# Strassen's block algorithm for the MLP's down product in a two-layer fp32 kernel on one core

## The chip, the core and the metric

The kernel runs on one core of a Trainium2 chip: TensorE (matmuls into PSUM), VectorE, ScalarE and GpSimd, each with its own instruction queue, and SyncE, whose queue issues most of the loads. The engines wait for each other through semaphores only. The metric is the time of one execution on the device in microseconds (us).

## What is computed

A block of an mLSTM mixer, stick-breaking attention and an MLP, then a block of sparse attention, on 512 tokens of width 1024 in fp32. The change touches the MLP of the first block alone:

```python
D_MODEL, SEQ, D_FF = 1024, 512, 4096
...
h2 = rms_norm(x, norm_mlp_g[l])
x = x + jnp.square(jax.nn.relu(h2 @ w_up[l])) @ w_down[l]
```

The result must have fp32's accuracy. The kernel reaches it with operands in a rounded format (fp32r): every matrix is split into a rounded part "hi" and the rest "lo", and a product is hi·hi + hi·lo + lo·hi, three matmuls.

## The kernel before

All weights are read as slabs of 1 MB, numbered through the program: 1024 rows x 256 columns, or (wide) 512 rows x 512 columns, a half of K. SyncE loads slab n into `w_raw[n % 2]` (L918 and L944), ScalarE rounds it into `w_hi[n % 2]` (`split_hi`, L550), VectorE forms the rest in `w_lo[n % 2]` (`split_lo`, L558: w_raw - w_hi), and TensorE uses both. Two slabs are in the works: slab n + 1 is split while TensorE works on n, and its rounding waits until TensorE has done with slab n - 1.

The MLP (`N_MLP`) runs in four rounds, one for each 1024 of the 4096 hidden columns, as a hardware loop on each engine (L944, L1134, L1450, L1695). A round has

- four up slabs. `mm_tile` (L581) makes two tiles of 128 hidden columns x 512 tokens of each, 24 matmuls a tile (8 steps of K, 3 parts), into the two banks of `ps_g` in turns. A tile is evacuated by ScalarE's Relu into `ev_t` (L732), VectorE's product with the tile itself, which gives the square, into `relu_t` (L819), ScalarE's rounding into `up_hi` (L734) and VectorE's rest into `up_lo` (L822). Only then is its bank free for the next tile but one.
- four wide down slabs, two halves of K for each 512 of the 1024 output columns. `mm_half` (L604) has the up activations as the stationary operand and adds into four banks, one for each 128 tokens; after the second half VectorE adds the bank to `x_sb` (L826).

Each engine does its work in program order: `act_slab` and `dve_slab` do the split of slab n + 1 first and then the evacuations of slab n. GpSimd has nothing to do in the MLP.

Behind the last round ScalarE squares the four blocks of 128 tokens of `x_sb` with a running sum (L886), VectorE forms the reciprocal root and the normalised `xn` (L900 to L908), and TensorE transposes it (`feature_tiles`, L632) for the next layer. Blocks 0 to 2 and block 3 are two parts of that.

## Time and profile before

| | us |
|---|---|
| median of 3 runs | 1376.48 |
| lowest, highest | 1375.53, 1377.55 |
| the profiled execution | 1374.61 |
| its span | 1372.9 |
| TensorE busy in the span | 1333.3 |
| VectorE, ScalarE, GpSimd busy | 669.1, 618.9, 201.9 |

The profile records one execution, instruction by instruction. Its page gives each engine's busy time, the granted clock of TensorE in 40 slices, the chain of waits that ended last, the costliest groups of instructions and the DMA issues; its trace can be asked for windows and timelines. A matmul is recorded for 0.39 us and the next starts 0.23 us behind it, since they are pipelined: their price is the distance between starts. "L558" is a line of the kernel. "1.26 <-ACT w_hi" behind an instruction is the engine's idle time before it and what ended it. An instruction that is held up after its start has the waiting time in its own duration.

### The profile page before, as it was taken

The numbers are of one execution on the slowest core, as the hardware profiler recorded it, in microseconds if no ns is written. First come the engines' busy times: TensorE is split into PE (matmuls) and PEld (weight loads), VectorE is DVE, ScalarE is ACT, GpSimd is POOL, SyncE is SP. The second block draws the span as 40 slices with busy tenths as digits, with TensorE's granted clock in tenths as the row PEclk, the third lists the DMA queues.
The fourth block names the chain that finished last, engine by engine and source line by source line (L and its number), as shares of the span: only waits on it lengthen the run. The fifth ranks groups of instructions, "written<-read, shape, count | busy, mean of one in ns | idle before, by whom it ended". The sixth has DMA issues, their size and how long they took to land.

```text
span 1372.9 us, 18095 instructions
## 1 busy us (share of the span) xinstructions
PE 1333.3 (97%) x7245; PEld 1115.1 (81%) x7245; DVE 669.1 (49%) x1093; ACT 618.9 (45%) x961; POOL 201.9 (15%) x265
## 2 busy tenths in 40 slices
PE   5999999999999999999999999999999999999998
PEld 4887777777778887888888888788899998989876
DVE  4753444344444545434434344431256767776563
ACT  5254554446766424323323223244334666666232
POOL 1101333261000000000000000002712333332000
PEclk9999999999999999999999999999999999999999
DMA  8747534494424322322232322272512222222321
GB/s 170 111 111 115 77 78 81 105 196 99 61 54 59 93 96 71 110 92 92 95 105 89 109 92 92 92 218 77 131 39 67 81 70 70 63 85 78 99 71 62
DMA packets 94807, 128.81 MB, mean 94 GB/s; under 512 B 5840, under 2 KB 70464, under 8 KB 94737
## 3 DMA queue, kind: packets, MB, share of 16 engines
q1 hardware_dynamic: 88528, 108.70, 32.1%
q0 software_dynamic: 6064, 18.83, 5.2%
...
## 4 chain that ended last, share of the span: by engine, by line
PE 86%; DVE 5%; DMA 4%; POOL 2%; ACT 2%; issue 1%; SPq 0%; DVEq 0%
PE ps_g L581 44%; PE ps_g L604 13%; PE ps_z L604 12%; PE ps_z L1236 3%; PE ps_z L1273 2%; PE ps_t L1308 2%; DMA w_raw<-in_w_in 2%; DMA bc<-stat_rows_dram 2%; PE ps_t L1045 1%; PE ps_t L1083 1%; DVE w_lo L558 1%; PE ps_z L1097 1%; POOL y_f L1907 1%; PE ps_t L1158 1%; PE ps_z L1121 1%
## 5 line engine op out<-in xcount | busy, mean ns | idle before, releaser
L558 DVE TENSOR_TENSOR w_lo<-w_raw,w_hi 128x2048 fp32r<-128x2048 f32 (+1 forms) x96 | 220.9, 2302 | 302.0 <-ACT w_hi L550 302.0
L581 PE MATMUL ps_g<-act_hi,w_hi 128*128 128x512 f32 x784 | 309.4, 395 | 7.8 <-DVE act_lo L697 5.3
L581 PE MATMUL ps_g<-act_hi,w_lo 128*128 128x512 f32 x784 | 306.3, 391 | 0.0
L581 PE MATMUL ps_g<-act_lo,w_hi 128*128 128x512 f32 x784 | 305.9, 390 | 0.0
L550 ACT ACTIVATE w_hi<-w_raw 128x2048 fp32r<-128x2048 f32 (+1 forms) x96 | 182.2, 1898 | 210.1 <-PE ps_g L604 189.0
L581 PEld LDWEIGHTS ps_g<-act_hi,w_hi 128*128 128x128 f32 x784 | 147.7, 188 | 41.0 <-DVE w_lo L558 5.8
L581 PEld LDWEIGHTS ps_g<-act_hi,w_lo 128*128 128x128 f32 x784 | 147.5, 188 | 31.3
L581 PEld LDWEIGHTS ps_g<-act_lo,w_hi 128*128 128x128 f32 x784 | 147.6, 188 | 29.5
L581 PE MATMUL ps_g<-w_hi,act_hi 128*128 128x256 f32 x320 | 93.4, 292 | 0.0
L581 PE MATMUL ps_g<-w_lo,act_hi 128*128 128x256 f32 x320 | 90.3, 282 | 0.0
L581 PE MATMUL ps_g<-w_hi,act_lo 128*128 128x256 f32 x320 | 90.2, 282 | 0.0
L1939 POOL TENSOR_SCALAR cmp_in_k<-pairk,vec 128x124 f32<-128x124 f32 x16 | 11.7, 749 | 518.0 <-ACT pairk L747 518.0
L1507 ACT ACTIVATE probs<-probs,rneg 128x128 f32<-128x128 f32 (+3 forms) x128 | 70.4, 551 | 13.8 <-DVE rneg L1761 12.8
L1959 POOL TENSOR_TENSOR q_parts<-qn,q_parts 64x512 fp32r<-64x512 f32 x32 | 42.0, 1312 | 139.6 <-ACT q_parts L1487 139.3
L581 PEld LDWEIGHTS ps_g<-w_hi,act_hi 128*128 128x128 f32 x320 | 61.1, 191 | 0.2 <-issue 0.2
L581 PEld LDWEIGHTS ps_g<-w_lo,act_hi 128*128 128x128 f32 x320 | 61.2, 191 | 0.0
L581 PEld LDWEIGHTS ps_g<-w_hi,act_lo 128*128 128x128 f32 x320 | 61.0, 191 | 0.0
L732 ACT ACTIVATE ev_t<-ps_g 128x512 f32<-128x512 f32 x32 | 19.2, 600 | 85.7 <-PE ps_g L581 85.7
L1757 DVE CUSTOM_DVE_ANT_0 probs<-ps_z,tile_t 128x128 f32<-128x128 f32 (+3 forms) x128 | 55.0, 485 | 5.7 <-PE ps_z L1236 3.2
L604 PE MATMUL ps_g<-w_hi,act_hi 128*128 128x512 f32 x128 | 49.9, 390 | 0.7 <-DVE act_lo L695 0.7
L819 DVE TENSOR_TENSOR relu_t<-ev_t,ps_g 128x512 f32<-128x512 f32 x32 | 22.0, 688 | 58.6 <-ACT ev_t L732 58.6
L604 PE MATMUL ps_z<-w_hi,act_hi 128*128 128x512 f32 x128 | 50.4, 394 | 0.0
...
## 6 DMA issues: line engine op xcount, KB each, us to landing
w_raw<-in_w_in SPq DMA_DIRECT2D x32, 1024.0 KB, 9.6
w_raw<-in_nsa_w_in SPq DMA_DIRECT2D x22, 1024.0 KB, 5.2
w_raw<-in_w_up SPq DMA_DIRECT2D x16, 1024.0 KB, 5.4
w_raw<-in_w_down SPq DMA_DIRECT2D x16, 1024.0 KB, 5.1
...
w_raw<-in_w_out SPq DMA_DIRECT2D x4, 1024.0 KB, 5.1
w_raw<-in_nsa_w_out SPq DMA_DIRECT2D x4, 1024.0 KB, 5.0
```

The source lines that it names most:

```text
L550: nc.scalar.activation(slab_view(w_hi[b], n), slab_view(w_raw[b], n), ACT.Copy).then_inc(hi_done, 1)
L558: nc.vector.tensor_tensor(slab_view(w_lo[b], n), slab_view(w_raw[b], n), slab_view(w_hi[b], n).bitcast(F32), ALU.subtract).then_inc(lo_don ...
L581: mm = nc.tensor.matmul(o, stationary, moving, start=(k == 0 and j == 0), stop=(k == KT - 1 and j == 2))
L604: mm = nc.tensor.matmul(bank(t), act[:, k, m], w[:, k - k0, :], start=(k == 0 and j == 0), stop=(k == KT - 1 and j == 2))
L732: nc.scalar.activation(ev_t[:, g, :], ps_g[:, g, :], ACT.Relu).then_inc(ev_act, 1)
L819: nc.vector.tensor_tensor(relu_t[:, g, :], ev_t[:, g, :], ps, ALU.mult)\
L1236: mm = nc.tensor.matmul(ps_z[:, at:at + w], q_parts[u % 2][:, b * P:(b + 1) * P], keys[u // 4 % 2][:, 0:w], start=(j == 0), stop=(j == 1))
L1273: mm = nc.tensor.matmul(ps_z[64 * e:64 * e + 64, CAUSAL + at * P:CAUSAL + (at + 1) * P], values[:, s, g * DH:(g + 1) * DH], probs_t[:, blo ...
L1308: mm = nc.tensor.transpose(ps_t[:, at:at + P], probs[u % 2][:, ROWS_AT[b] + s * P:ROWS_AT[b] + (s + 1) * P], ident)
L1507: ins = nc.scalar.activation(p, p, ACT.Exp, bias=rneg[:, u % 2, b:b + 1], accum_out=rsum[:, u % 2, b:b + 1])
L1757: ins = nc.vector.tensor_tensor_reduce(probs[u % 2][:, at:at + w], ps_z[:, at:at + w], tile_t[u % 2][:, S - w:S], 1.0, -3.0e38, ALU.add, A ...
L1959: nc.gpsimd.tensor_tensor(q_parts[u % 2][64 - half:128 - half, :], qn[half:half + 64, 4 * (h // 8) + h % 4, :], q_parts[u % 2][half:half + ...
```

## The change

The down product of each round is done with Strassen's algorithm in Winograd's form. The round's up activations A (512 tokens x 1024) and weights B (1024 x 1024) are cut into four blocks each: A11, A12, A21, A22 (first index: half of the tokens; second: half of K) and B11 to B22 (half of K; half of the output columns). Instead of 8 block products there are seven:

- M1 = A11·B11, M2 = A12·B21
- S1 = A21 + A22, S2 = S1 - A11, S3 = A11 - A21, S4 = A12 - S2
- T1 = B12 - B11, T3 = B22 - B12, T2 = T3 + B11, T4 = B21 - T2
- M5 = S1·T1, M4 = A22·T4, M6 = S2·T2, M7 = S3·T3, M3 = S4·B22

The output's blocks are x11 += M1 + M2, x12 += M1 + M6 + M5 + M3, x21 += M1 + M6 + M7 + M4, x22 += M1 + M6 + M7 + M5. (T4 and M4 have their signs such that these hold.) The products run in the order M1, M2, M5, M4, M6, M7, M3, each with 24 matmuls (2 blocks of 128 tokens, 4 steps of K, 3 parts).

Each product has a slab of weights of its own that is split as before, so a round has 11 slabs, four for up and seven for down, in place of 8. The four raw down slabs are loaded into buffers of their own (`down_raw`). New work in a round:

- GpSimd: T3, T1 and T2 (2048 elements in each partition), released by the split of up slab 2, by the one before, and by the split of M1; S3, S2, S4 (1024 elements), released by `mixed_1` and then by one another; six additions of 512 elements to `x_sb` behind M6 and M7.
- VectorE: S1 (`mix1`, 1024 elements), T4 (2048), the rests of S1 to S4 (1024 each), 12 additions of 512 elements from PSUM (8 before), seven splits (4 before). The rests of A11 and A12 alone are half as wide at the first four up tiles.
- ScalarE: seven roundings of weights (4 before), two copies of M1 out of PSUM, the roundings of S1 to S4.

The hardware loops are written out. The blocks of tokens are normalised for the next layer in the order 2, 3, 0, 1.

```diff
+M1, M2, M5, M4, M6, M7, M3 = range(7)
+PRODUCTS = 7
...
+        up_raw = [sb(f"up_raw{j}", [P, HALF_K, S], at=arena + 2 * K16 + 8192 * j) for j in range(2)]
+        down_raw = [sb(f"down_raw{i}", [P, HALF_K, WIDE], at=arena + 3 * K16 + 8192 * i) for i in range(4)]
+        mix1 = sb("mix1", [P, HALF_K, HALF_S], at=arena + 5 * K16)
+        prod1 = sb("prod1", [P, 2, WIDE], at=arena + 5 * K16 + 4096)
+        prod16 = sb("prod16", [P, 2, WIDE], at=arena + 5 * K16 + 8192)
+        prod167 = sb("prod167", [P, 2, WIDE], at=arena + 5 * K16 + 12288)
...
+        NORM_BLOCKS = ((0, 1, 2, 3), (0, 1, 2, 3), (2, 3, 0, 1))
...
+        def down_operand(p):
+            j = 0 if p in (M1, M5, M6, M3) else 1
+            half = slice(0, HALF_S) if p in (M1, M2, M6, M7) else slice(HALF_S, S)
+            return (up_parts[j][0][:, :, half], up_parts[j][1][:, :, half])
+        def down_bank(p, i):
+            return {M1: ps_z[:, 512 * i:512 * i + 512], M2: ps_z[:, 512 * i:512 * i + 512],
+                    M5: (ps_z, ps_t)[i][:, 1024:1536], M3: (ps_z, ps_t)[i][:, 1024:1536],
+                    M4: ps_g[:, i, :],
+                    M6: ps_t[:, 512 * i:512 * i + 512], M7: ps_t[:, 512 * i:512 * i + 512]}[p]
...
+            def down_product(q, p):
+                n = N_MLP + MLP_SLABS * q + 4 + p
+                up0 = tile_of[n - p - 4]
+                pe.wait_ge(lo_done, n + 1)
+                hi, lo = down_operand(p)
+                wh, wl = slab_view(w_hi[n % 2], n), slab_view(w_lo[n % 2], n)
+                if p in (M1, M2):
+                    for k in range(HALF_K):
+                        wait_tile_free(pe, up0 + HALF_K * p + k)
+                elif p != M4:
+                    pe.wait_ge(mix_lo, 4 * q + {M5: 1, M6: 2, M7: 3, M3: 4}[p])
+                for i in range(2):
+                    if p == M1 and q:
+                        pe.wait_ge(prod_added, added(q - 1, M2, i))
+                    elif p == M2:
+                        pe.wait_ge(prod_copied, 2 * q + i + 1)
+                    elif p == M5 and q:
+                        pe.wait_ge(prod_added, added(q - 1, M3, i))
+                    elif p == M6 and q:
+                        pe.wait_ge(prod_added, added(q - 1, M7, i))
+                    elif p == M7:
+                        pe.wait_ge(prod_added, added(q, M6, i))
+                    elif p == M3:
+                        pe.wait_ge(prod_added, added(q, M5, i))
+                    first, last_ = p not in (M2, M7, M3), True
+                    for k in range(HALF_K):
+                        m = slice(i * P, (i + 1) * P)
+                        for j, (act, w) in enumerate(((hi, wh), (hi, wl), (lo, wh))):
+                            mm = nc.tensor.matmul(down_bank(p, i), act[:, k, m], w[:, k, :],
+                                                  start=(first and k == 0 and j == 0),
+                                                  stop=(k == HALF_K - 1 and j == 2), skip_group_check=True)
+                    mm.then_inc(prod_done, 1)
...
+            def mixed_hi(q, s):
+                src, dst = ((mix1[:], up_parts[0][0][:, :, HALF_S:S]),
+                            (up_raw[0][:, :, 0:HALF_S], up_parts[0][0][:, :, 0:HALF_S]),
+                            (up_raw[0][:, :, HALF_S:S], up_parts[1][0][:, :, 0:HALF_S]),
+                            (up_raw[1][:, :, 0:HALF_S], up_parts[0][0][:, :, HALF_S:S]))[s]
+                if s == 0:
+                    act.wait_ge(mixed_1, q + 1)
+                else:
+                    act.wait_ge(mixed_up, 3 * q + (2, 1, 3)[s - 1])
+                    act.wait_ge(prod_done, prod_count(q, (M1, M2, M5)[s - 1], 1))
+                nc.scalar.copy(dst, src).then_inc(mix_hi, 1)
+            for q in range(4):
+                n = N_MLP + MLP_SLABS * q
+                for j in range(4):
+                    act_slab(act, n + j)
+                for p in range(PRODUCTS):
+                    split_hi(act, n + 4 + p + 1)
+                    if p == M1:
+                        for i in range(2):
+                            act.wait_ge(prod_done, prod_count(q, M1, i))
+                            if q:
+                                act.wait_ge(prod_added, added(q - 1, M7, i))
+                            nc.scalar.copy(prod1[:, i, :], down_bank(M1, i)).then_inc(prod_copied, 1)
+                            if i == 0:
+                                mixed_hi(q, 0)
+                    elif p in (M5, M4, M6):
+                        mixed_hi(q, {M5: 1, M4: 2, M6: 3}[p])
+            def x_there(b):
+                if b >= 2:
+                    act.wait_ge(prod_merged, 6 * 3 + 2 + 2 * (b - 1))
+                else:
+                    act.wait_ge(prod_added, added(3, M3, b))
+            act_rms(act, 2, x_there)
...
+            def mixed_lo(q, s):
+                src, j, half = ((mix1[:], 0, slice(HALF_S, S)),
+                                (up_raw[0][:, :, 0:HALF_S], 0, slice(0, HALF_S)),
+                                (up_raw[0][:, :, HALF_S:S], 1, slice(0, HALF_S)),
+                                (up_raw[1][:, :, 0:HALF_S], 0, slice(HALF_S, S)))[s]
+                dve.wait_ge(mix_hi, 4 * q + s + 1)
+                nc.vector.tensor_tensor(up_parts[j][1][:, :, half], src, up_parts[j][0][:, :, half].bitcast(F32),
+                                        ALU.subtract).then_inc(mix_lo, 1)
+            def add_product(q, p, i):
+                dve.wait_ge(prod_done, prod_count(q, p, i))
+                ps = down_bank(p, i)
+                if p in (M6, M7):
+                    if p == M6:
+                        dve.wait_ge(prod_copied, 2 * q + i + 1)
+                        if q:
+                            dve.wait_ge(prod_merged, 6 * (q - 1) + 2)
+                    elif q:
+                        dve.wait_ge(prod_merged, 6 * q)
+                    dst = (prod16 if p == M6 else prod167)[:, i, :]
+                    nc.vector.tensor_tensor(dst, prod1[:, i, :], ps, ALU.add).then_inc(prod_added, 1)
+                    return
+                x = x_block(*{M2: (0, 0), M5: (1, 1), M4: (1, 0), M3: (0, 1)}[p], i)
+                if p == M3:
+                    dve.wait_ge(prod_merged, 6 * q + i + 1)
+                elif p in (M5, M4) and q:
+                    dve.wait_ge(prod_merged, 6 * q)
+                nc.vector.tensor_tensor(x, x, ps, ALU.add).then_inc(prod_added, 1)
+            for q in range(4):
+                n = N_MLP + MLP_SLABS * q
+                for j in range(4):
+                    dve_slab(dve, order, n + j)
+                dve.wait_ge(ev_dve, dve_count[tile_of[n + 4]])
+                nc.vector.tensor_tensor(mix1[:], up_raw[0][:, :, HALF_S:S], up_raw[1][:, :, HALF_S:S], ALU.add)\
+                    .then_inc(mixed_1, 1)
+                for p in range(PRODUCTS):
+                    split_lo(dve, n + 4 + p + 1)
+                    if p == M1:
+                        mixed_lo(q, 0)
+                        dve.wait_ge(mixed_w, 3 * q + 3)
+                        dve.wait_ge(lo_done, n + 4 + M2 + 1)
+                        nc.vector.tensor_tensor(down_raw[1][:], down_raw[1][:], down_raw[0][:], ALU.subtract)\
+                            .then_inc(mixed_b21, 1)
+                    else:
+                        add_product(q, p, 0)
+                        if p in (M5, M4, M6):
+                            mixed_lo(q, {M5: 1, M4: 2, M6: 3}[p])
+                        add_product(q, p, 1)
...
+            for q in range(4):
+                n = N_MLP + MLP_SLABS * q
+                b11, b12, b22 = (down_raw[i][:] for i in (0, 2, 3))
+                t3 = slab_view(w_raw[raw_of[n + 4 + M7]], n + 4 + M7)
+                a11, a21 = up_raw[0][:, :, 0:HALF_S], up_raw[0][:, :, HALF_S:S]
+                a12 = up_raw[1][:, :, 0:HALF_S]
+                for i in (3, 2):
+                    pool.wait_ge(down_in[i], 16 * (q + 1))
+                pool.wait_ge(lo_done, n + 3)
+                nc.gpsimd.tensor_tensor(t3, b22, b12, ALU.subtract).then_inc(mixed_w, 1)
+                pool.wait_ge(down_in[0], 16 * (q + 1))
+                pool.wait_ge(mixed_w, 3 * q + 1)
+                nc.gpsimd.tensor_tensor(b12, b12, b11, ALU.subtract).then_inc(mixed_w, 1)
+                pool.wait_ge(lo_done, n + 4 + M1 + 1)
+                pool.wait_ge(mixed_w, 3 * q + 2)
+                nc.gpsimd.tensor_tensor(b11, t3, b11, ALU.add).then_inc(mixed_w, 1)
+                pool.wait_ge(mixed_1, q + 1)
+                nc.gpsimd.tensor_tensor(a21, a11, a21, ALU.subtract).then_inc(mixed_up, 1)
+                pool.wait_ge(mixed_up, 3 * q + 1)
+                nc.gpsimd.tensor_tensor(a11, mix1[:], a11, ALU.subtract).then_inc(mixed_up, 1)
+                pool.wait_ge(mixed_up, 3 * q + 2)
+                nc.gpsimd.tensor_tensor(a12, a12, a11, ALU.subtract).then_inc(mixed_up, 1)
+                for i in range(2):
+                    pool.wait_ge(prod_added, added(q, M6, i))
+                    x = x_block(0, 1, i)
+                    nc.gpsimd.tensor_tensor(x, x, prod16[:, i, :], ALU.add).then_inc(prod_merged, 1)
+                for i in range(2):
+                    pool.wait_ge(prod_added, added(q, M7, i))
+                    for column in range(2):
+                        x = x_block(1, column, i)
+                        nc.gpsimd.tensor_tensor(x, x, prod167[:, i, :], ALU.add).then_inc(prod_merged, 1)
```

How instructions move. VectorE, from the fourth up slab of a round to the down product; before (`w_lo` is the rest of a weight slab; REGISTER_ALU belongs to the loop):

```order
L558 TENSOR_TENSOR w_lo_57<-w_raw_53,w_hi_55 128x2048 [waits hi_done]
L668 REGISTER_ALU
L819 TENSOR_TENSOR relu_t<-ev_t,ps_g 128x512 [waits ev_act]
L668 REGISTER_ALU
L822 TENSOR_TENSOR up_lo<-relu_t,up_hi 128x512 [waits ev_act]
L557 REGISTER_ALU
L558 TENSOR_TENSOR w_lo_56<-w_raw_52,w_hi_54 128x2048 [waits hi_done]
L557 REGISTER_ALU
L558 TENSOR_TENSOR w_lo_57<-w_raw_53,w_hi_55 128x2048 [waits hi_done]
```

and after, in the same place (down_raw_101, 102, 103 hold B11, B21 and B12, later T2, T4 and T1):

```order
L886 TENSOR_TENSOR up_lo<-up_raw_100,up_hi 128x512 [waits ev_act]
L1915 TENSOR_TENSOR mix_105<-up_raw_99,up_raw_100 128x1024 [waits ev_dve]
L615 TENSOR_TENSOR w_lo_56<-down_raw_102,w_hi_54 128x2048 [waits hi_done]
L1886 TENSOR_TENSOR up_lo<-mix_105,up_hi 128x4x256 [waits mix_hi]
L1923 TENSOR_TENSOR down_raw_102<-down_raw_102,down_raw_101 128x2048 [waits lo_done,mixed_w]
L615 TENSOR_TENSOR w_lo_57<-down_raw_103,w_hi_55 128x2048 [waits hi_done]
L1908 TENSOR_TENSOR x_sb<-x_sb,ps_z 128x512 [waits prod_done] x2
```

Between the last evacuation of an up tile and the split of the third product's weights stand now, besides the split of the second product's, S1, the rest of S1 and T4. GpSimd, in the place of the MLP, before:

```order
L1844 AFFINE_SELECT sp_t<-sp_t 128x128 [waits b_sp] x2
L1844 AFFINE_SELECT sp_t<-sp_t 128x128 x2
L1939 TENSOR_SCALAR cmp_in_k<-pairk,vec 128x124 [waits tile_free0,tile_free1]
L1939 TENSOR_SCALAR cmp_in_k<-pairk,vec 128x124 x15
L1939 TENSOR_SCALAR cmp_in_v<-pairv,vec 128x124 [waits cmp_ready,tile_free0,tile_free1]
```

and after, the first of four rounds (up_raw_99 holds A11 and A21, up_raw_100 A12 and A22, w_raw_53 T3, prod_107 M1 + M6, prod_108 M1 + M7, to which M6 is added in PSUM):

```order
L2076 AFFINE_SELECT sp_t<-sp_t 128x128 x2
L2174 TENSOR_TENSOR w_raw_53<-down_raw_104,down_raw_103 128x2048 [waits lo_done,down_in2,down_in3]
L2177 TENSOR_TENSOR down_raw_103<-down_raw_103,down_raw_101 128x2048 [waits mixed_w,down_in0]
L2180 TENSOR_TENSOR down_raw_101<-w_raw_53,down_raw_101 128x2048 [waits mixed_w,lo_done]
L2182 TENSOR_TENSOR up_raw_99<-up_raw_99 128x4x256 [waits mixed_1]
L2184 TENSOR_TENSOR up_raw_99<-mix_105,up_raw_99 128x4x256 [waits mixed_up]
L2186 TENSOR_TENSOR up_raw_100<-up_raw_100,up_raw_99 128x4x256 [waits mixed_up]
L2190 TENSOR_TENSOR x_sb<-x_sb,prod_107 128x512 [waits prod_added] x2
L2195 TENSOR_TENSOR x_sb<-x_sb,prod_108 128x512 [waits prod_added]
```

GpSimd, which had no instruction in the MLP, has twelve in each round.

## Rows read from the trace of the kernel before

**Rows 1.** The page, part 1: busy us (share of the span) xinstructions
```profile
PE 1333.3 (97%) x7245; PEld 1115.1 (81%) x7245; DVE 669.1 (49%) x1093; ACT 618.9 (45%) x961; POOL 201.9 (15%) x265
```

**Rows 2.** Window table inside the MLP: stretch, us, busy us (count) by engine
```profile
600.00:850.00 250.00, 250.00 (x1105) 207.01 (x1104) 100.14 (x93) 72.22 (x71) 0.00 (x0) 1.00 0.30 96
```

**Rows 3.** Chain of waits before the MLP: start us, us, what
```profile
519.34 5.44 PE ps_z L604 x24
```

**Rows 4.** Timeline between two MLP rounds: start us, us, engine, line, operation
```profile
625.92 0.39 PE L581 MATMUL ps_g<-act_hi,w_hi 128*128 128x512 f32 x1
626.12 1.92 ACT L550 ACTIVATE w_hi<-w_raw 128x2048 fp32r<-128x2048 f32 x1 [8.96 <-PE ps_g L604]
...
628.07 2.29 DVE L558 TENSOR_TENSOR w_lo<-w_raw,w_hi 128x2048 fp32r<-128x2048 f32 x1 [1.26 <-ACT w_hi L550]
```

**Rows 5.** Timeline, ScalarE then VectorE, end of a round's first up slab
```profile
637.00 0.60 ACT L732 ACTIVATE ev_t<-ps_g 128x512 f32<-128x512 f32 x1 [3.46 <-PE ps_g L581]
638.36 0.62 ACT L734 CAST up_hi<-relu_t 128x512 fp32r<-128x512 f32 x1 [0.75 <-DVE relu_t L819]
...
637.64 0.69 DVE L819 TENSOR_TENSOR relu_t<-ev_t,ps_g 128x512 f32<-128x512 f32 x1 [3.37 <-ACT ev_t L732]
...
640.83 2.29 DVE L558 TENSOR_TENSOR w_lo<-w_raw,w_hi 128x2048 fp32r<-128x2048 f32 x1 [1.13 <-ACT w_hi L550]
```

**Rows 6.** Lines that split weight slabs: count, ns least/median/most
```profile
L558 DVE TENSOR_TENSOR w_lo<-w_raw,w_hi x96: 1226/2293/3367, 17.3 to 1347.2; 128x2048 fp32r<-128x2048 f32 x94, 128x1024 fp32r<-128x1024 f32 x2
...
L550 ACT ACTIVATE w_hi<-w_raw x96: 1045/1916/1992, 15.3 to 1345.2; 128x2048 fp32r<-128x2048 f32 x94, 128x1024 fp32r<-128x1024 f32 x2
```

**Rows 7.** GpSimd's tensor_tensor by line: count, ns least/median/most, shape
```profile
L1888 POOL TENSOR_TENSOR den_sum<-den_sum,decay x8: 459/792/797, 130.3 to 241.6; 128x128 f32<-128x128 f32 x8
...
L1907 POOL TENSOR_TENSOR y_f<-y_f,bc x8: 1272/1516/3332, 275.5 to 301.3; 128x512 f32<-128x512 f32 x8
...
L1959 POOL TENSOR_TENSOR q_parts<-qn,q_parts x32: 1282/1291/1980, 1023.2 to 1256.9; 64x512 fp32r<-64x512 f32 x32
```

**Rows 8.** Timeline pieces, GpSimd and VectorE, at 277 to 301 us
```profile
277.25 1.78 DVE L1647 SCALAR_TENSOR_TENSOR q_b<-q_b,gq_s,bc 128x512 f32<-128x512 f32 x1
...
278.44 1.74 POOL L1907 TENSOR_TENSOR y_f<-y_f,bc 128x512 f32<-128x512 f32 x1
...
296.72 4.59 POOL L1907 TENSOR_TENSOR y_f<-y_f,bc 128x512 f32<-128x512 f32 x2
...
296.79 3.37 DVE L558 TENSOR_TENSOR w_lo<-w_raw,w_hi 128x2048 fp32r<-128x2048 f32 x1 [9.01 <-ACT w_hi L550]
...
297.98 3.33 POOL L1907 TENSOR_TENSOR y_f<-y_f,bc 128x512 f32<-128x512 f32 x1
```

**Rows 9.** Timeline at 1063 us: GpSimd beside a VectorE operation on PSUM
```profile
1061.83 2.63 POOL L1969 TENSOR_TENSOR k_lo<-ks,k_hi 64x512 fp32r<-64x512 f32 x2 [2.91 <-ACT k_hi L1500]
...
1063.30 0.69 DVE L1757 CUSTOM_DVE_ANT_0 probs<-ps_z,tile_t 128x512 f32<-128x512 f32 x1
```

**Rows 10.** The page, part 6: DMA issues, KB each, us to landing
```profile
w_raw<-in_w_down SPq DMA_DIRECT2D x16, 1024.0 KB, 5.1
```

**Rows 11.** TensorE's timeline after a gap; window table (PEclk third from the end)
```profile
20.44 0.47 PE L581 MATMUL ps_g<-act_hi,w_hi 128*128 128x512 f32 x1 [3.64 <-DVE act_lo L697]
...
21.46 0.59 PE L581 MATMUL ps_g<-act_lo,w_hi 128*128 128x512 f32 x1
...
24.83 0.43 PE L581 MATMUL ps_g<-act_hi,w_hi 128*128 128x512 f32 x1
...
20.00:24.00 4.00, 3.56 (x11) 0.69 1.02 77
```

**Rows 12.** Timeline, TensorE and ScalarE, at the end of the MLP rounds
```profile
886.82 0.39 PE L604 MATMUL ps_g<-w_hi,up_lo 128*128 128x512 f32 x1
...
888.15 1.04 ACT L886 ACTIVATE xn<-x_sb 128x1024 f32<-128x1024 f32 x1
...
889.30 0.55 PE L632 MATMUL ps_z<-cst,xn 128*128 128x128 f32 x3 [2.09 <-DVE xn L908]
```

More of the change, by code:

```diff
@@ L471, in program @@
             tile_of[n] = len(kinds)
+            if slabs[n][4] == "down":
+                continue
             if k_half(n) is None:
@@ L623, in feature_bank, with feature_tiles @@
             return (ps_z, ps_t)[k // 3][:, k % 3 * 512:(k % 3 + 1) * 512]
-        def feature_tiles(pe, n, src, block_ready, between=None, before=None):
+        def feature_tiles(pe, n, src, block_ready, between=None, before=None, blocks=range(TB), late=None):
             t0 = norm_tile_of[n]
```

292 lines of the change are left out of this document (179 added, 113 removed).

## The prediction

> **What bounds the kernel now.** I read the page first: TensorE is busy 97% of the span, VectorE 49%, ScalarE 45%, GpSimd 15% [rows 1]. Then the stretch that the change touches, the four MLP rounds from 538.7 us to 887 us. In the window table 250 us out of the middle of it are 250.00 us of TensorE work, with GpSimd at 0.00 and the granted clock at 1.00 [rows 2]. So TensorE alone sets the time here, at one tile of 24 matmuls in 5.44 us [rows 3], 0.2267 us a matmul; a round has 384 of them, 87.05 us.
>
> What keeps the other engines off the path is slack. At a slab's boundary ScalarE rounds the next weight slab (1.92 us) and VectorE then forms its rest (2.29 us); with the handovers the slab is ready 4.44 us behind the boundary (625.92 to 628.07 + 2.29 [rows 4]), while TensorE works 10.88 us on a slab. Behind an up slab its last tile is evacuated first (Relu 0.60, product 0.69, rounding 0.62 us, then a rest as long as the product) and the split runs from 636.80 (625.92 + 10.88) to 643.12, 6.32 us [rows 5]. ScalarE has up to 8.96 us to wait for TensorE [rows 4].
>
> **TensorE's part of the change.** Seen as blocks (tokens halved, K halved, output columns halved) the down product of a round is 8 block products of 24 matmuls (2 token tiles, 4 steps of K, 3 parts): 192. Seven block products are 168. So 24 matmuls, 5.44 us, leave each round and 21.8 us the kernel. The matmul has the same shape as before, hence its price.
>
> **The slack after it.** A product lasts 2 x 12 x 0.2267 = 5.44 us where a slab lasted 10.88. The pair of split halves still takes 4.44 us: 1.0 us of slack is left at each product instead of 6.4. So every further operation of VectorE and ScalarE in the product part has to be placed. Durations I use: 2048 elements 1.92 us on ScalarE and 2.29 on VectorE [rows 4]; 1024 elements 1.05 and 1.23 (the least of the two lines that split slabs, which are the half-width ones) [rows 6]; 512 elements 0.60 and 0.69 [rows 5].
>
> **GpSimd's operations.** Its tensor_tensor takes at least 0.46 us for 128 elements and 1.27 us for 512 [rows 7]: 0.19 us and 2.11 ns an element. Worked out from these: 1024 elements 2.35 us, 2048 elements 4.5 us. The trace has none so long; the slower end is the median of the 512-element line in the sparse attention, 1291 ns, at that rate throughout: 2.52 ns an element [rows 7], 2.6 and 5.2 us; the faster end has no fixed part, 2.11 ns throughout, 2.2 and 4.3 us. I take the line through the two minima, which are undisturbed. The Trainium skill (GPSIMD Engine Reference, Performance versus the Vector engine) gives 4497 ns for 2048 fp32 elements, no row here shows it; by it the sum would stay.
>
> **What decides: GpSimd and VectorE don't run side by side on these operations.** At 296 us GpSimd is in the midst of four multiplications of 512 elements. VectorE's split starts at 296.79, just behind one of them (296.72), and is recorded with 3.37 us instead of 2.29: it waits 1.08 us, until that one is done, then runs. GpSimd's next operation, begun at 297.98, takes 3.33 instead of 1.27: it waits 2.1 us until the split has ended at 300.16 [rows 8]. From 277.25 on the two alternate one by one: VectorE's 0.75 us operation is recorded with 1.78, and GpSimd's with 1.74, each behind one of the other engine [rows 8]. Whereas VectorE's operations with one operand in PSUM ran inside a GpSimd pair (1063.30, 0.69 us for 512 elements, no longer than elsewhere) [rows 9]. So: operations with two SBUF inputs exclude each other, whole instruction by whole instruction, in turns; adds from PSUM are free. The Trainium skill (SBUF — State Buffer, SBUF: two separate sides) calls it an exclusive lock and not a bandwidth split; these rows agree with it. If the ports were shared by bandwidth, as the skill's page says they are not, the sum would be that of rival A below.
>
> **The round, step by step**, in us from its first matmul; boundaries between engines 0.03 to 0.1.
> - Up part. GpSimd's first weight difference starts when slab 2 of the round is split: TensorE's tile 1 ends at 10.88, the split 6.2 later (a 256-wide rounding and rest are 0.2 shorter each), 17.1. It holds until 21.7 (4.5). VectorE's rest of tile 2 (ready 18.3) waits and runs to 22.1; the second difference runs 22.1 to 26.6; the rest of tile 3 waits from 23.7 to 26.6 and ends 27.05. TensorE needs that bank for tile 5 at 27.20: no stall, by 0.15 us. The third runs 39.2 to 43.7 behind M1's split and delays the rest of tile 6 to 44.4, that of tile 7 hardly (46.5). M1 starts on time at 43.52: 0.
> - M1 to M2. M2's split needs tile 7 evacuated first: VectorE's mix1 ends 47.75 (46.5 + 1.23), ScalarE's rounding of M2 47.7. M2 should start at 48.96. From 47.8 VectorE has in its queue: split M2 (2.29), rest of mix1 (1.23), difference for M4 (2.29), split M5 (2.29) = 8.1 us. GpSimd is released by mix1 at the same instant for its three sums of up activations, each waiting for the one before: 3 x 2.35 = 7.05 us. All seven have two SBUF inputs. In turns, whoever is first, all three GpSimd sums are done before split M5 starts: 47.8 + 8.1 + 7.05 = 62.95. M2 starts at 50.1 or, if GpSimd wins the first turn, at 52.5, and ends 55.5 or 57.9; M5 starts at 63.0 either way instead of 54.4. **Stall 8.6 us a round**, +34.4 us.
> - M5, M4, M6, M7, M3. VectorE's load per 5.44 us is split 2.29, rest 1.23, two adds 1.38 = 4.9 us. From M6's start T: split M7 to T + 4.44, add, rest to 6.4, GpSimd's first add to x (1.27) to 7.7, split M3 7.7 to 10.0, needed at 10.88; GpSimd to 11.25; two adds; one GpSimd add holds until 13.87, so the next slab's split ends 16.16, needed at 16.32. It fits, with 0.16 us: 0.
> - Loads. 8 MB a round as before, 5.1 us each [rows 10]; they are issued at the splits of the round before and land before use, also in the first round, where four of them are queued at once. 0.
>
> **The clock.** At 20.44 us TensorE had idled 3.64 us; between 21.46 and 24.83 only eight matmuls start, 0.42 us apart instead of 0.227, the lower of the two levels (granted clock 0.69 in 20 to 24 us) [rows 11]: 1.6 us lost. A gap of 7.5 us (or two, of 3.5 and 5) before M5 will do the same: +1.6 a round, +6.4 us. Bounds: 0, and 2 x 1.6 if both gaps do it.
>
> **The end of the rounds.** Now the squares of blocks 0 to 2 are done beside TensorE, and the first transpose starts 2.09 us after its last matmul (886.82 + 0.39 to 889.30) [rows 12]: VectorE's add 0.69, then 1.4 for mean, root, reciprocal and the first normalisation. After the change blocks 2 and 3 are complete only with GpSimd's six adds to x, of which the last ends 2.3 us behind M3's end (held once by the split of the next slab); then two squares (2 x 1.25: 1.04 [rows 12] and the reading of the sum) and the 1.4: first transpose 6.2 us behind. +4.1 us, once. At least 1.9 if nothing holds the adds.
>
> **Sum**, against the profiled execution (1374.6 us in all, its span 1372.9): -21.8 + 34.4 + 6.4 + 4.1 = +23.1. The three runs have their median 1.9 us above that execution, so 1376.5 + 23.1 = **1399.6 us**.
>
> **Rivals.**
> - A: the exclusion doesn't bite in this place (the sums find the gaps between VectorE's operations, or my reading of rows 8 holds for those forms only). Then split M5 ends at 47.8 + 8.1 = 55.9: stall 1.5 us a round, no clock loss, tail +1.9: -21.8 + 6 + 1.9 = -13.9, **1362.6 us, faster**. It decides below a stall of about 4.4 us a round (21.8 - 4.1 over four), that is with one GpSimd sum in the way, not three. For it: VectorE and ScalarE are half idle. Against: rows 8 show both engines waiting, to the hundredth.
> - B: only two of the three sums get in before split M5, or the clock doesn't fall: 2.35 x 4 = 9.4 less, or 6.4 less: 1390 to 1393. It needs VectorE to win two turns running; at 277.25 to 278.95 it won none.
> - C: GpSimd is at its slower rate. The first two differences then end 1.4 us later, tile 5 waits 1.3 us a round, the three sums 0.8 more: +8.4, **1408**. Double clock loss would add 6.4 to the forecast likewise.
> - D: the split of a further product comes late (slack 0.16 us behind M3): some tenths a round, within the range.
>
> **Chances.** Forecast with D 0.58, B 0.14, C and the double clock loss 0.18, A 0.10. Range 1384 to 1411: it takes in B and C with their bounds and leaves out A and a sum of all bad ends. A measurement of this kernel can tell about 0.2%, 2.7 us. Faster 0.10, same 0.02, slower 0.88.
>
> **What would show it.** In the profile after: tiles of 5.44 us still; per round two gaps of TensorE before M2 and before M5, together near 8.6 us, ended by VectorE's w_lo; recorded VectorE operations in that place longer than 2.29 by whole GpSimd operations, and GpSimd's 1024-element sums longer than 2.35; granted clock below 1 behind the gap; VectorE's busy time up far more than its elements. Wrong if w_lo stays 2.29 us beside a busy GpSimd (then A), if the gap stands at another product, or if the up tiles wait (then C).

## The result, and the profile after

The changed kernel takes **1398.74 us** (median of 4 runs, 1395.45 to 1400.6), the kernel before beside it 1377.01. The ratio is 1.0162, with a 95% interval from 1.0146 to 1.0177: slower, and 0.9 us from the predicted 1399.6. The difference of the two medians is +21.7 us where +23.1 was forecast; the kernel before ran 0.5 us above the 1376.5 that the forecast started from. The profiled execution took 1395.45 us, the shortest of the four, and its span is 1393.7.

The page, part 1, of the changed kernel (busy us, share of the span, instructions; compare [rows 1]):

```profile
PE 1324.2 (95%) x7149; PEld 1103.4 (79%) x7149; DVE 799.2 (57%) x1145; ACT 657.3 (47%) x997; POOL 347.8 (25%) x313
```

TensorE has 96 instructions fewer, as it should. VectorE's busy time is up by 130 us, and GpSimd's by 146. Since a waiting instruction has its wait in its duration, both are more than the new work.

The best measure of the change is a stretch that holds all of it and nothing else: from the MLP's first matmul to the first matmul of the next layer. TensorE's timeline of the kernel before, start us, us, then the instruction and its wait:

```profile
538.73 0.50 PE L581 MATMUL ps_g<-act_hi,w_hi 128*128 128x512 f32 x1 [0.80 <-DVE act_lo L697]
...
894.15 0.47 PE L581 MATMUL ps_g<-act_hi,w_hi 128*128 128x512 f32 x1 [0.89 <-DVE act_lo L697]
```

and of the changed one:

```profile
537.75 0.47 PE L638 MATMUL ps_g<-act_hi,w_hi 128*128 128x512 f32 x1 [0.89 <-DVE act_lo L759]
...
917.32 0.47 PE L638 MATMUL ps_g<-act_hi,w_hi 128*128 128x512 f32 x1 [0.89 <-DVE act_lo L759]
```

355.42 us before and 379.57 after: **+24.15**. What lies outside this stretch took 1017.5 us before and 1014.1 after, so that the two profiled executions are only 20.8 us apart. Over the profiled executions of all the kernels here, whose code doesn't differ there, it lies between 1014.1 and 1019.0. The missing 3.4 us are within that scatter of single executions, and the experiments below are compared by their stretch as well as by their time.

Where TensorE waited in the MLP of the changed kernel (waits of TensorE, 530 to 915 us: us in total, times, longest):

```profile
PE ps_z L1274 <- DVE w_lo L615: 28.6, 8, 6.4
PE ps_z L689 <- DVE xn L976: 7.9, 2, 5.7
PE ps_g L638 <- DVE up_lo L886: 1.1, 4, 0.3
```

Eight waits for a weight split, two a round, at M2 and at M5. In the second round (its first matmul starts at 629.45) TensorE's timeline has them so:

```profile
679.90 0.50 PE L1274 MATMUL ps_z<-w_hi,up_hi 128*128 128x512 f32 x1 [0.77 <-DVE w_lo L615]
...
692.02 0.79 PE L1274 MATMUL ps_z<-w_hi,up_hi 128*128 128x512 f32 x1 [6.37 <-DVE w_lo L615]
692.61 0.63 PE L1274 MATMUL ps_z<-w_lo,up_hi 128*128 128x512 f32 x1
693.03 0.63 PE L1274 MATMUL ps_z<-w_hi,up_lo 128*128 128x512 f32 x1
...
695.98 0.39 PE L1274 MATMUL ps_z<-w_hi,up_hi 128*128 128x512 f32 x1
```

M2 starts at 50.45 in the round (forecast 50.1, or 52.5) and M5 at 62.57 (forecast 63.0). Behind the second wait the matmuls start some 0.43 us apart (the first two 0.59) instead of 0.23, until 695.98. The windows of the same kernel (stretch, us, busy us of PE, PEld, DVE, ACT, POOL with counts, granted clock, DMA share, GB/s; compare [rows 2]):

```profile
540.00:900.00 360.00, 330.36 (x1409) 268.45 (x1408) 266.05 (x180) 136.12 (x133) 138.56 (x44) 0.96 0.26 83
...
692.00:696.00 4.00, 3.98 (x10) 3.15 (x11) 3.36 (x3) 0.00 (x0) 0.00 (x0) 0.51 0.67 219
```

The clock is 0.51 behind the gap, the lower of the two levels (1.2 GHz), and 0.96 in the mean of the MLP, where it was 1.00.

**Why the split is late** stands on the two other engines in the same place, VectorE first, then GpSimd:

```profile
676.35 1.22 DVE L1915 TENSOR_TENSOR mix<-up_raw,up_raw 128x1024 f32<-128x1024 f32 x1
677.56 2.29 DVE L615 TENSOR_TENSOR w_lo<-down_raw,w_hi 128x2048 fp32r<-128x2048 f32 x1
679.77 3.43 DVE L1886 TENSOR_TENSOR up_lo<-mix,up_hi 128x1024 fp32r<-128x1024 f32 x1
683.12 4.48 DVE L1923 TENSOR_TENSOR down_raw<-down_raw,down_raw 128x2048 f32<-128x2048 f32 x1
687.52 4.44 DVE L615 TENSOR_TENSOR w_lo<-down_raw,w_hi 128x2048 fp32r<-128x2048 f32 x1
...
677.65 4.47 POOL L2182 TENSOR_TENSOR up_raw<-up_raw 128x1024 f32<-128x1024 f32 x1 [3.99 <-DVE mix L1915]
682.19 3.25 POOL L2184 TENSOR_TENSOR up_raw<-mix,up_raw 128x1024 f32<-128x1024 f32 x1
685.53 4.28 POOL L2186 TENSOR_TENSOR up_raw<-up_raw,up_raw 128x1024 f32<-128x1024 f32 x1
```

Read them as one sequence of turns. VectorE's split of M2 comes first (2.29, unhindered). GpSimd's S3, begun at 677.65, waits for it until 679.8 and ends at 682.12. VectorE's rest of S1 (1.22 by itself, recorded with 3.43) waits for S3 and ends at 683.20; S2 waits for it, T4 (2.29 by itself, 4.48 here) for S2, S4 for T4, and the split of M5 (4.44) for S4. Seven operations, strictly in turns, from 677.56 to 691.96: 14.4 us. TensorE starts M5 0.06 us later.

### The profile page after: what moved, and what is told of

It is laid out like the page before. It is cut to its first block, busy times and chain, and to the rows that moved or that the text cites. A ratio compares the mean times of both kernels' runs of the same rounds, so it can differ in the third digit from the quotient of the medians.

```text
span 1393.7 us, 17752 instructions
## 1 busy us (share of the span) xinstructions
PE 1324.2 (95%) x7149; PEld 1103.4 (79%) x7149; DVE 799.2 (57%) x1145; ACT 657.3 (47%) x997; POOL 347.8 (25%) x313
## 4 chain that ended last, share of the span: by engine, by line
PE 81%; DVE 10%; ACT 3%; DMA 2%; issue 2%; POOL 1%; SPq 0%; DVEq 0%; ACTq 0%; POOLq 0%
PE ps_g L638 42%; PE ps_g L661 7%; PE ps_z L661 7%; PE ps_t L1274 4%; DVE w_lo L615 3%; PE ps_z L1387 3%; PE ps_z L1424 3%; PE ps_t L1459 2%; PE ps_z L1274 2%; DMA w_raw<-in_w_in 2%; PE ps_g L1274 2%; DVE down_raw L1923 1%; DVE up_lo L886 1%; PE ps_t L1156 1%; PE ps_t L1194 1%
## 5 line engine op out<-in xcount | busy, mean ns | idle before, releaser
L615 DVE TENSOR_TENSOR w_lo<-w_raw,w_hi 128x2048 fp32r<-128x2048 f32 (+1 forms) x84 | 196.6, 2340 | 230.0 <-ACT w_hi L607 230.0
L607 ACT ACTIVATE w_hi<-w_raw 128x2048 fp32r<-128x2048 f32 (+1 forms) x84 | 159.2, 1896 | 116.8 <-PE ps_g L661 62.1
L607 ACT ACTIVATE w_hi<-down_raw 128x2048 fp32r<-128x2048 f32 x24 | 46.0, 1916 | 71.5 <-PE ps_t L1274 47.3
L615 DVE TENSOR_TENSOR w_lo<-down_raw,w_hi 128x2048 fp32r<-128x2048 f32 x24 | 66.9, 2788 | 13.1 <-ACT w_hi L607 13.1
L1274 PE MATMUL ps_z<-w_hi,up_hi 128*128 128x512 f32 x96 | 42.1, 438 | 28.6 <-DVE w_lo L615 28.6
L886 DVE TENSOR_TENSOR up_lo<-up_raw,up_hi 128x256 fp32r<-128x256 f32 (+1 forms) x32 | 54.5, 1702 | 18.6 <-ACT up_hi L797 18.6
L2174 POOL TENSOR_TENSOR w_raw<-down_raw,down_raw 128x2048 f32<-128x2048 f32 x4 | 18.4, 4607 | 167.8 <-DVE w_lo L615 167.8
```

The lines of the kernel that those rows point to most:

```text
L607: nc.scalar.activation(slab_view(w_hi[b], n), slab_view(raw(n), n), ACT.Copy).then_inc(hi_done, 1)
L615: nc.vector.tensor_tensor(slab_view(w_lo[b], n), slab_view(raw(n), n), slab_view(w_hi[b], n).bitcast(F32), ALU.subtract).then_inc(lo_done, 1)
L886: nc.vector.tensor_tensor(up_parts[j][1][:, k, cols], up_raw[j][:, k, cols], up_parts[j][0][:, k, cols].bitcast(F32), ALU.subtract).then_i ...
L1274: mm = nc.tensor.matmul(down_bank(p, i), act[:, k, m], w[:, k, :], start=(first and k == 0 and j == 0), stop=(k == HALF_K - 1 and j == 2), ...
```

## Experiments

In 1 to 5 all else is as in the changed kernel; 6 and 7 change the rearranged kernel of 4. "Stretch" is the distance defined above, in one profiled execution of each.

| | median us | ratio to before, 95% interval | stretch us |
|---|---|---|---|
| before | 1376.05 to 1377.01 | | 355.42 |
| changed | 1398.74 | 1.0162 [1.0146, 1.0177] | 379.57 |
| sums on one element | 1364.48 | 0.9912 [0.9896, 0.9929] | 346.99 |
| memsets in their place | 1364.40 | 0.9915 [0.9898, 0.9932] | 345.74 |
| sums behind the split of M5 | 1376.09 | 0.9993 [0.9983, 1.0003] | 357.19 |
| rearranged | 1364.35 | 0.9913 [0.9897, 0.9930] | 345.50 |
| the same again | 1364.10 | 0.9914 [0.9897, 0.9930] | 345.54 |
| sums on VectorE | 1383.18 | 1.0058 [1.0042, 1.0073] | 365.83 |
| rearranged, other parts of the normalisation | 1363.97 | 0.9910 [0.9897, 0.9924] | 346.81 |
| rearranged, last additions on VectorE | 1364.94 | 0.9912 [0.9895, 0.9929] | 344.65 |

**1. The three sums made small.**

```diff
-nc.gpsimd.tensor_tensor(a21, a11, a21, ALU.subtract).then_inc(mixed_up, 1)
+nc.gpsimd.tensor_tensor(a21[:, 0:1, 0:1], a11[:, 0:1, 0:1], a21[:, 0:1, 0:1],
+                        ALU.subtract).then_inc(mixed_up, 1)
```

and likewise S2 and S4.

> The changed kernel with GpSimd's three sums of up activations (S3, S2, S4) done on one element in each partition in place of 1024; the rest of them is left out, every wait stays. Theory L (two-input operations of GpSimd and VectorE exclude each other whole, so the three sums lengthen VectorE's chain before the fifth matrix product M5 by their own 3 x 2.35 us): M5 starts 1.1 + 0.4 us late a round instead of about 8.6, the clock doesn't fall there, recorded w_lo of that place is 2.29 us: 1398.7 - 4 x 7.1 - 6.4 = about 1364 us, faster than before. Theory V (VectorE's own 8.1 us of queue and ScalarE's order behind it make the gap, GpSimd is beside the path): gap and time stay, 1394 to 1399.

Measured: 1364.48 us. Of the eight waits for `w_lo` only the four of 0.77 us at M2 are left. VectorE and GpSimd in the second round:

```profile
669.44 2.29 DVE L615 TENSOR_TENSOR w_lo<-down_raw,w_hi 128x2048 fp32r<-128x2048 f32 x1
671.65 1.22 DVE L1886 TENSOR_TENSOR up_lo<-mix,up_hi 128x1024 fp32r<-128x1024 f32 x1
672.79 2.29 DVE L1923 TENSOR_TENSOR down_raw<-down_raw,down_raw 128x2048 f32<-128x2048 f32 x1
674.99 2.28 DVE L615 TENSOR_TENSOR w_lo<-down_raw,w_hi 128x2048 fp32r<-128x2048 f32 x1
...
669.53 2.25 POOL L2182 TENSOR_TENSOR up_raw<-up_raw 128x1 f32<-128x1 f32 x1 [3.98 <-DVE mix L1915]
671.86 1.06 POOL L2184 TENSOR_TENSOR up_raw<-mix,up_raw 128x1 f32<-128x1 f32 x1
673.00 2.12 POOL L2186 TENSOR_TENSOR up_raw<-up_raw,up_raw 128x1 f32<-128x1 f32 x1
```

All that VectorE does has its own length again. GpSimd's subtractions of a single element still wait out each operation of VectorE (2.25, 1.06, 2.12 us). So the turns go by instruction, whatever its size. VectorE loses only as much as GpSimd holds, and the M5 wait is GpSimd's three sums. It doesn't yet tell whether GpSimd's being busy or its reading is what excludes.

**2. GpSimd busy, but without inputs.** Each sum is three memsets of its target, one after the other.

```diff
-nc.gpsimd.tensor_tensor(a21, a11, a21, ALU.subtract).then_inc(mixed_up, 1)
+nc.gpsimd.memset(a21, 0.5).then_inc(filled, 1)
+pool.wait_ge(filled, 6 * q + 1)
...
+nc.gpsimd.memset(a21, 0.5).then_inc(mixed_up, 1)
```

> The changed kernel with each of GpSimd's three sums replaced by three memsets of the same 1024-element target, one waiting for the other (the sums are left out). GpSimd is then busy about as long in the same place, but reads nothing from SBUF. Theory L in its narrow form (only a GpSimd operation that reads SBUF excludes VectorE's two-input operations): VectorE's w_lo stays 2.29 us beside the memsets, as with the narrow sums, about 1364 us. Theory L in its wide form (any GpSimd operation with SBUF in it excludes): w_lo lengthened by whole memsets, time between 1370 and 1400 by their length. Theory V: 1394 to 1399.

Measured: 1364.40 us. GpSimd beside VectorE's T4:

```profile
672.43 2.29 DVE L1924 TENSOR_TENSOR down_raw<-down_raw,down_raw 128x2048 f32<-128x2048 f32 x1
...
672.20 0.96 POOL L2189 MEMSET up_raw<- 128x1024 f32 x1
...
674.23 0.96 POOL L2193 MEMSET up_raw<- 128x1024 f32 x1
```

Nine memsets of 0.95 to 0.96 us follow one another, eight of them across VectorE's operations with two SBUF inputs and the last beside its additions from PSUM. That one takes 0.95 us like the others, and VectorE's operations have their own lengths of 2.29 and 1.22 us. The order and the handovers are those of the sums, with six more, and GpSimd is busy for 9 x 0.96 = 8.6 us, so neither its load nor the added handovers cost TensorE anything: what excludes VectorE is a GpSimd operation that reads SBUF. That a memset is shorter than a sum isn't the reason, since the sums on one element of experiment 1 are shorter still (each ends some 0.05 us behind the VectorE operation it waited for) and do wait. All the GpSimd operations that waited here have two inputs; none with a single input was tried. The Trainium skill (SBUF — State Buffer, SBUF: two separate sides) has an operation of VectorE with two SBUF inputs excluded "only against a GpSimd op that reads SBUF"; this run agrees.

**3. The same sums, later.** GpSimd waits for the split of M5 before the first of them. Nothing is left out.

```diff
                 pool.wait_ge(mixed_1, q + 1)
+                pool.wait_ge(lo_done, n + 4 + M5 + 1)
```

> The changed kernel, nothing left out; GpSimd begins its three sums only when the weights of M5 are split (one wait more). Theory L: the same 7 us of exclusion are paid behind that split, where VectorE has about 0.5 us to spare in each product: M5 is late by 1.5 us instead of 8.6, the split for M6 by some 2.7, no gap is longer than 3.6 us, so little clock loss: 4.3 us of gaps a round, 4 x (81.6 + 4.3 - 87.05) + 4.1 = about 0 against before, 1373 to 1381. Theory V: the M5 gap stays as it is, as in the changed kernel, and sums that come later can only add: 1398 or more.

Measured: 1376.09 us, the time of the kernel before. TensorE's waits, 530 to 915 us:

```profile
PE ps_t L1274 <- DVE w_lo L615: 8.6, 4, 2.2
...
PE ps_z L1274 <- DVE w_lo L615: 3.1, 4, 0.8
```

The same seven operations, 22.7 us off the time by their order alone. M5's wait of 6.4 is gone; a new one of 2.2 us stands at M6, four times. GpSimd's S3 now takes 2.42 us by itself (679.79), but S2 (682.29) is recorded with 4.32, since the split of M4 (681.96, 2.41) is in its way. The rounding and rest of S2 are later, and VectorE, in its order, stands in front of M6's split and waits for them. The ten executions of this kernel lie from 1373.48 to 1378.27 us: the four with a granted clock of 0.992 or 0.993 took at most 1374.17, the six with 0.988 to 0.991 at least 1375.69. The clock behind this gap probably falls more often in some than in others; in the profiled one (1376.49) it fell in the last round alone. Moving the sums helps, but three in a row find no hole long enough.

**4. Rearranged.** S3 goes into the up part (released by the up activations that it reads, into `prod167`, which is free then). The weight sums are T1 = B12 - B11, T2 = B22 - T1, T3 = T2 - B11, T4 = B21 - T2, and GpSimd does T4 too, all of them ahead of M2. S2 waits for the split of M5, S4 for that of M4. The loads of the next round are issued accordingly. Nothing is left out.

```diff
+                nc.gpsimd.tensor_tensor(b12, b12, b11, ALU.subtract).then_inc(mixed_w, 1)
...
+                nc.gpsimd.tensor_tensor(t2, b22, b12, ALU.subtract).then_inc(mixed_w, 1)
...
+                nc.gpsimd.tensor_tensor(s3, a11, a21, ALU.subtract).then_inc(mixed_up, 1)
...
+                nc.gpsimd.tensor_tensor(t3, t2, b11, ALU.subtract).then_inc(mixed_w, 1)
...
+                nc.gpsimd.tensor_tensor(b11, b21, t2, ALU.subtract).then_inc(mixed_w, 1)
                 pool.wait_ge(mixed_1, q + 1)
+                pool.wait_ge(lo_done, n + 4 + M5 + 1)
                 pool.wait_ge(mixed_up, 3 * q + 1)
                 nc.gpsimd.tensor_tensor(a11, mix1[:], a11, ALU.subtract).then_inc(mixed_up, 1)
+                pool.wait_ge(lo_done, n + 4 + M4 + 1)
                 pool.wait_ge(mixed_up, 3 * q + 2)
                 nc.gpsimd.tensor_tensor(a12, a12, a11, ALU.subtract).then_inc(mixed_up, 1)
```

> A rearranged version of the changed kernel, nothing left out: GpSimd forms T1 in the first up slab, T2 = B22 - T1 and T3 = T2 - B11 in places of the up part between VectorE's rests, S3 before the last up slab into a buffer of its own, and T4 in place of VectorE; in the product part only S2 (behind M5's split) and S4 (behind M4's) are left to it. Theory L: in the up part all exclusion falls into slack; M2 is late by 1.1 us, M4 and M6 by 0.2 or so: 82.9 us a round against 87.05, -16.4, and +4.1 at the end: 1376.5 - 12.3 = about 1364, faster than both kernels. Theory V: without T4 VectorE's queue before M5 is 5.8 us in place of 8.1, so a gap of about 6.3 us would be left, and the rest of the clock loss: about 1385 to 1390.

Measured: 1364.35 us, and 1364.10 when it ran again (experiment 7): **12 us faster than the kernel before**, and 34 than the changed one. TensorE's waits and the window of the MLP:

```profile
PE ps_z L1275 <- DVE w_lo L613: 3.1, 4, 0.8
```

```profile
540.00:900.00 360.00, 349.34 (x1538) 286.07 (x1537) 262.57 (x197) 153.68 (x158) 144.75 (x52) 1.00 0.30 95
```

GpSimd has more to do than in the changed kernel (144.75 against 138.56 us busy in this stretch, with its waits), and the clock is back at 1.00. VectorE and GpSimd behind M1:

```profile
673.07 2.29 DVE L613 TENSOR_TENSOR w_lo<-down_raw,w_hi 128x2048 fp32r<-128x2048 f32 x1 [0.63 <-ACT w_hi L605]
...
675.49 2.40 POOL L2191 TENSOR_TENSOR up_raw<-mix,up_raw 128x1024 f32<-128x1024 f32 x1 [10.38 <-issue]
681.52 2.42 POOL L2194 TENSOR_TENSOR up_raw<-up_raw,up_raw 128x1024 f32<-128x1024 f32 x1 [3.62 <-DVE w_lo L613]
```

M5's split has its 2.29 us, and the two sums left sit behind a split each.

**5. The sums on VectorE.** Around its rest of S1 and behind its T4:

```diff
+                        nc.vector.tensor_tensor(a21, a11, a21, ALU.subtract).then_inc(mixed_up, 1)
                         mixed_lo(q, 0)
...
+                        nc.vector.tensor_tensor(a11, mix1[:], a11, ALU.subtract).then_inc(mixed_up, 1)
...
+                        nc.vector.tensor_tensor(a12, a12, a11, ALU.subtract).then_inc(mixed_up, 1)
```

> The changed kernel, nothing left out, with the three sums of up activations on VectorE in place of GpSimd, at the places of its queue where GpSimd's turns fell. The exclusion is gone, VectorE's own work is 3 x 1.13 us more. Theory L: M5's split ends after 11.2 us of VectorE's queue instead of 14.4 measured; two gaps of 1.2 and 3.5 us a round: 86.3 us against 87.05, +4.1 at the end: 1377 to 1378 if the clock stays up behind a gap of 3.5 us, up to 1384 if it falls each time. A rival, that the sums' place before M5's split and not the engine's pace matters: as the changed kernel, 1397.

Measured: 1383.18 us, 15.6 less than with the sums on GpSimd, but slower than before. TensorE waits 3.21 us at M5, and the window behind it has the lower clock:

```profile
685.38 0.67 PE L1274 MATMUL ps_z<-w_hi,up_hi 128*128 128x512 f32 x1 [3.21 <-DVE w_lo L615]
```

```profile
686.00:690.00 4.00, 4.00 (x13) 3.14 (x12) 2.72 (x2) 0.00 (x0) 0.00 (x0) 0.63 0.92 262
```

It fell in all four rounds behind this gap. In the stretch, against before: -21.8 for the matmuls, 4 x 3.37 for M5, 4 x 1.04 for M2, 2.0 in the up tiles, 0.3 elsewhere, 4 x 1.7 for the clock and 5.0 at the end make +9.9 to set against +10.4 measured. Without the clock's 6.8 us the time would be 1376.4, at the 1377 expected with the clock up: M5's gap and the end would still use up the gain of the seven products. The sums stand ahead of M5's split as in the changed kernel, so their place alone doesn't make the gap of 6.4 us: they hold VectorE for 3 x 2.4 = 7.2 us when GpSimd does them and for 3.7 when VectorE does, 3.5 less, and the gap is 3.2 shorter.

**6. The end of the rounds: fewer blocks in the first part.**

```diff
-((0, 3), (3, 4))
+((0, 2), (2, 4))
...
-(2, 3, 0, 1)
+(2, 0, 1, 3)
```

The rearranged kernel, with blocks 2 and 0 as the first part and 1 and 3 as the second, where blocks 2, 3, 0 were the first.

> The rearranged kernel of the last call with the last normalisation in two pairs of token blocks, (2, 0) and (1, 3), in place of (2, 3, 0) and (1): block 3, which GpSimd completes last, is no longer in the first part. If GpSimd's last additions are what the end of the rounds waits for, the first transpose starts some 2.9 us earlier and the next layer 2 to 3.5 us earlier: 1361 to 1362.5. If VectorE's or ScalarE's chain behind it sets the time, it stays at 1364.

Measured: 1363.97 us, no gain. TensorE at the end of the rounds, first in the rearranged kernel, then in this one:

```profile
876.91 0.66 PE L687 MATMUL ps_z<-cst,xn 128*128 128x128 f32 x2 [5.66 <-DVE xn L974]
...
882.86 0.47 PE L636 MATMUL ps_g<-act_hi,w_hi 128*128 128x512 f32 x1 [0.89 <-DVE act_lo L757]
```

```profile
876.83 0.66 PE L687 MATMUL ps_z<-cst,xn 128*128 128x128 f32 x2 [3.27 <-DVE xn L974]
...
878.68 0.69 PE L687 MATMUL ps_z<-cst,xn 128*128 128x128 f32 x2 [0.77 <-DVE xn L974]
...
885.08 0.47 PE L636 MATMUL ps_g<-act_hi,w_hi 128*128 128x512 f32 x1 [0.89 <-DVE act_lo L757]
```

The first transpose comes 2.4 us sooner behind the last matmul, as expected, and from there the next layer is 8.25 us away instead of 5.95. (In the first round of this execution TensorE also waited 1.7 us for `up_lo` where the rearranged kernel had 0.35, hence its longer stretch.)

**7. The end of the rounds: the last additions on VectorE.** In the last round VectorE does M7's four additions to `x_sb`; the parts are blocks 2, 3 and blocks 0, 1. The rearranged kernel ran beside it.

```diff
+                        if (q, p) == (3, M7):
...
+                                    nc.vector.tensor_tensor(x, x, prod167[:, i, :], ALU.add)\
+                                        .then_inc(prod_merged, 1)
```

> The rearranged kernel (e4), with one thing more at the end of the rounds: in the last round the four additions of M7's part to x (512 elements, two SBUF inputs) are done by VectorE behind its additions of M7 from PSUM instead of by GpSimd, and blocks 2 and 3 are a first part of the normalisation, blocks 0 and 1 a second. Nothing is left out. In the rearranged kernel GpSimd's fourth addition ended 1.9 us behind TensorE's last matmul, and the first transpose started 5.66 us behind it. Theory: that end is a chain of VectorE, GpSimd and ScalarE in which the last additions bind. VectorE does the four in 4 x 0.65 = 2.6 us, from 866.6 to 869.2 on the rearranged kernel's clock, the next slab's split then ends at 871.5 and its two last additions at 872.9, which is when its mean and root follow: the first transpose should start some 3 us behind the last matmul and the time be 2 to 2.5 us less than the rearranged kernel's, 1361.5 to 1362.5 us. Rival, from what the other parts of the normalisation gave (a first transpose 2.4 us earlier, and the next layer's first matmul no earlier): the last part and the transposes at the lower clock bind, and the time stays at 1364.

> The rearranged kernel (e4) once more, unchanged, to stand beside the one with the last additions on VectorE on the same chip: 1364.4 us, 0.991 of the kernel before.

Measured: 1364.94 and 1364.10 us. The first transpose now starts 2.56 us behind the last matmul instead of 5.66, so GpSimd's additions did bind it. The stretch is 0.9 us shorter, which the time doesn't show. The windows of this kernel while TensorE transposes:

```profile
876.00:880.00 4.00, 3.23 (x16) 2.83 (x15) 2.31 (x5) 0.73 (x3) 0.00 (x0) 0.50 0.40 138
880.00:884.00 4.00, 3.11 (x19) 2.90 (x18) 1.09 (x2) 1.81 (x4) 0.00 (x0) 0.75 0.00 0
```

and of the rearranged one:

```profile
876.00:880.00 4.00, 3.09 (x16) 3.00 (x17) 3.06 (x6) 1.01 (x3) 0.00 (x0) 0.57 0.00 0
880.00:884.00 4.00, 3.11 (x24) 2.72 (x22) 2.04 (x4) 2.76 (x5) 0.00 (x0) 1.00 0.00 0
```

With the long gap the transposes run at the lower clock for their first 3 us (to 879.9) and then at the full one; with the short gap and a wait of 0.77 us among them, for 6.5 us (875.58 to 882.1). That gives back 2.3 of the 3.1 us: about 1.0 by the wait between the two parts (the third pair of transposes starts 1.41 us behind the second, not 0.42) and 1.3 by the clock. So the rival named beforehand fits. Whether the clock stayed down longer for the shorter gap or for that wait, no run tells apart; experiment 6 has both too.

## Why the prediction was right, and where its steps were off

Terms of the sum for the stretch, from the distances between starts of matmuls (what exceeds 0.227):

| | forecast us | measured us |
|---|---|---|
| 24 matmuls fewer a round | -21.8 | -21.8 |
| up tiles | 0 | +2.0 |
| M2 and M5 late | +34.4 | +30.3 |
| clock behind M5's gap | +6.4 | +7.9 |
| other products | 0 | +0.3 |
| end of the rounds | +4.1 | +4.9 |
| sum | +23.1 | +23.6 (of 24.15) |

- **The turns.** Seven exclusive operations, all of GpSimd's sums ahead of M5's split: confirmed, even to the strict alternation, which left rival B (VectorE wins two turns running) without a case. M2 started at the earlier of its two forecast times. The size was 4.1 us too high, 3 of it from one source: 8.1 + 7.05 us were summed from durations, but an instruction starts some 0.1 us before the one ahead of it is recorded as ended (679.77 against 677.56 + 2.29), so that the seven took 14.4 and not 15.15. Rival A gave 1362.6 for an exclusion that doesn't bite; with the sums on one element the kernel took 1364.5.
- **The up tiles: a wrong step.** The prediction had the rest of tile 2 end at 22.1 us in the round and compared the rest of tile 3 with the start of tile 5, "no stall, by 0.15 us". But tile 2's bank is needed by tile 4, at 21.76. Its own number gave a stall of 0.3. GpSimd, VectorE and TensorE there:

```profile
646.62 4.60 POOL L2174 TENSOR_TENSOR w_raw<-down_raw,down_raw 128x2048 f32<-128x2048 f32 x1 [15.04 <-DVE w_lo L615]
...
647.78 3.73 DVE L886 TENSOR_TENSOR up_lo<-up_raw,up_hi 128x256 fp32r<-128x256 f32 x1 [0.47 <-ACT up_hi L797]
...
651.65 0.47 PE L638 MATMUL ps_g<-act_hi,w_hi 128*128 128x512 f32 x1 [0.26 <-DVE up_lo L886]
```

  The rest of 256 elements, held for all of the 4.60 us of GpSimd's difference, ends at 651.51, 22.06 in the round; TensorE should have gone on at 651.23. With what the restart costs it is 0.5 us a round. Tile 5 itself didn't wait. By the prediction's own sign ("if the up tiles wait (then C)") this would have pointed to rival C, and it doesn't: the next point has GpSimd's durations.
- **GpSimd's durations** were read from a line through two minima [rows 7]: 2.35 and 4.5 us; they are 2.40 (where nothing hinders them, rearranged kernel) and 4.60. The slower end, rival C, is out. The Trainium skill's 4497 ns for 2048 elements (GPSIMD Engine Reference, Performance versus the Vector engine) is 2% below this form's 4.60.
- **The clock** fell once a round as forecast from [rows 11], behind the long gap and not behind M2's. It took back 8 to 10 matmuls at 0.43 us, and 1.7 to 2.2 us instead of 1.6.
- **M4 to M3** fitted in their 5.44 us each with no wait for `w_lo`; so did the loads.
- **The end.** GpSimd's last addition ends at 907.41, 1.9 us behind the last matmul (905.48; forecast 2.3), and the squares of two blocks follow, as forecast:

```profile
900.35 7.06 POOL L2195 TENSOR_TENSOR x_sb<-x_sb,prod 128x512 f32<-128x512 f32 x4 [2.83 <-DVE prod L1901]
...
907.45 1.06 ACT L953 ACTIVATE xn<-x_sb 128x1024 f32<-128x1024 f32 x1 [3.36 <-POOL x_sb L2195]
...
911.22 0.66 PE L689 MATMUL ps_z<-cst,xn 128*128 128x128 f32 x2 [5.74 <-DVE xn L976]
```

  TensorE idles 5.7 us against the forecast 6.2, +3.65 over [rows 12]. The missed part lies behind: the transposes ran at the lower clock at first, and the next layer started 1.25 us later still.

That the total came out within a microsecond is partly luck, because misses cancel. In the stretch they are 4.1 us too much at M2 and M5 and 4.6 too little in the up tiles, the clock, the other products and the end; 0.5 us of the stretch stays unassigned. The medians then differ by 2.4 us less than the stretches (+21.7 against +24.15), and the kernel before ran 0.5 us above the forecast's base. The mechanism is shown: the gap goes when GpSimd's sums are small (1), when they read nothing (2), or when they stand elsewhere (3, 4), and shrinks when VectorE does them (5).

Two things stay open. M2's 0.77 us is in every version, since S1 and the rounding of M2's weights both end just before it; no run tried to part them. And why M6's gap of 2.2 us in experiment 3 lowered the clock in the last round alone isn't explained by the gap's length.
